# Score levels' inputs between value copies, and the order in which sparse attention opens

## The reference

```python
# branch A: gated linear attention
inter = einsum('blhk,bhkv->blhv', qb * exp(cum), state)
scores = einsum('bthk,btshk,bshk->btsh', qb, exp(cum[t] - cum[s]), kb)   # within a chunk
k_dec = kb * exp(tot - cum)
state = state * exp(tot) + einsum('blhk,blhv->bhkv', k_dec, vb)
# branch C: mLSTM over qc, kc, vc; each head ends in a norm and a gate
# branch B: sparse attention
cq, ckv = rms(cq, dsa_norm_q), rms(ckv, dsa_norm_kv)      # ranks 256 and 128
q_idx = einsum('bsr,rhd->bshd', cq, w_qi) * 32 ** -0.5    # 8 index heads of 32
I = sum_h w[t,h] * relu(q_idx[t,h] . k_idx[s])            # causal
sel = top_k(I, 128)                                       # keys of each token
p = softmax(q_lat . ckv[sel] - slope * dist);  o = p @ ckv[sel]
# then gates * branches, @ w_o, router, 6 of 64 experts a token plus a shared one
```

## Time and profile before

| | us |
|---|---|
| median of 3 runs | 1441.36 (1438.7 to 1453.93) |
| profiled execution, its own time | 1441.15 |
| its span | 1439.3 |
| PE busy | 1318.4 (92%) |
| DVE busy | 1038.8 (72%) |
| ACT busy | 778.6 (54%) |

### The profile page before, as it was taken

The page is one execution under the profiler, slowest core; times in us unless marked ns, Lnnn a source line. Parts: engine busy times, 40 slices in busy tenths (PEclk is TensorE's granted clock), DMA queues, the critical chain, the costliest instruction groups (busy, mean ns, idle before and its releaser), DMA issues.

```text
span 1439.3 us, 19410 instructions
## 1 busy us (share of the span) xinstructions
PE 1318.4 (92%) x6398; PEld 1011.6 (70%) x6398; DVE 1038.8 (72%) x1302; ACT 778.6 (54%) x952; POOL 431.0 (30%) x321
## 2 busy tenths in 40 slices
PE   4897999996898889998997999999999999999986
PEld 1586788563654458888965888788887888887842
DVE  1539685774997717444576988888988999998927
ACT  3613431433334533222314888788888888888811
POOL 1100000013221000000001666566656666665610
PEclk8999999998999999999998999999999999999998
DMA  8333312003216242334227999999999999999856
GB/s 297 102 102 124 118 59 74 29 15 109 66 60 226 74 153 85 103 99 147 73 94 259 361 383 394 383 385 367 357 373 376 347 350 359 357 370 336 309 215 252
DMA packets 126617, 314.57 MB, mean 219 GB/s; under 512 B 24229, under 2 KB 61418, under 8 KB 118122
## 3 DMA queue, kind: packets, MB, share of 16 engines
q1 hardware_dynamic: 108282, 288.73, 55.7%
q0 software_dynamic: 18288, 25.21, 4.9%
HBM read 316.49 MB, written 38.80 MB: 247 GB/s over the span
## 4 chain that ended last, share of the span: by engine, by line
PE 61%; DMA 15%; DVE 11%; issue 5%; ACT 4%; POOL 2%; SPq 1%; POOLq 0%; DVEq 0%; ACTq 0%
PE bank L898 15%; PE bank L1284 9%; PE bank L903 8%; PE bank L1312 7%; DMA arena<-h_dram,tok_of 7%; DMA ring<-in_exp_w_up 5%; PE bank L1288 4%; PE bank L1271 3%; DVE arena L2070 2%; DVE top L2069 2%; DMA arena<-in_ada_w 1%; PE bank L1353 1%; PE bank L1141 1%; POOL tok_of L780 1%; PE bank L845 1%
## 5 line engine op out<-in xcount | busy, mean ns | idle before, releaser
L2324 DVE TENSOR_TENSOR ring_parts<-ring,arena_parts 128x2048 fp32r<-128x2048 f32 x186 | 424.0, 2290 | 64.2 <-ACT arena_parts L1664 63.5
L1664 ACT ACTIVATE arena_parts<-ring 128x2048 fp32r<-128x2048 f32 x186 | 356.7, 1927 | 51.8 <-DMA ring<-in_exp_w_up 47.4
L1284 PE MATMUL bank<-arena_parts,oTA_parts 128*128 128x512 f32 x496 | 200.2, 404 | 2.9 <-DVE oTC_parts L2340 1.9
L1284 PE MATMUL bank<-arena_parts,oTC_parts 128*128 128x512 f32 x496 | 195.0, 393 | 0.0
L1312 PE MATMUL bank<-arena_parts,oTB_parts 128*128 128x512 f32 x496 | 162.2, 409 | 5.1 <-DVE ring_parts L2324 5.1
L793 POOL DMA_INDIRECT y_dram<-arena,row_of x62 | 98.6, 1591 | 183.7 <-ACT arena L1691 181.2
L898 PE MATMUL bank<-hT_parts,ring_parts 128*128 128x512 f32 x344 | 143.3, 416 | 5.4 <-ACT arena L1569 3.7
L768 POOL DMA_INDIRECT arena<-h_dram,tok_of x61 | 127.3, 2088 | 54.5 <-POOL tok_of L780 51.0
L898 PE MATMUL bank<-x_parts,ring_parts 128*128 128x512 f32 x344 | 136.7, 397 | 0.0
L1288 PE MATMUL bank<-ring_parts,oTA_parts 128*128 128x512 f32 x496 | 133.7, 392 | 0.0
L1396 ACT ACTIVATE ring_parts<-ring 128x2048 fp32r<-128x2048 f32 (+1 forms) x38 | 64.8, 1710 | 118.1 <-DMA ring<-in_w_in 71.1
(11 more groups left out here) (420 smaller groups left out, 2276.7 us busy)
## 6 DMA issues: line engine op xcount, KB each, us to landing
ring<-in_exp_w_gate SPq DMA_DIRECT2D x124, 512.0 KB, 5.3
ring<-in_exp_w_up SPq DMA_DIRECT2D x124, 512.0 KB, 9.9
ring<-in_exp_w_down SPq DMA_DIRECT2D x62, 1024.0 KB, 9.8
ring<-in_w_in SPq DMA_DIRECT2D x25, 1024.0 KB, 5.4
ring<-in_ada_w SPq DMA_DIRECT2D x16, 1024.0 KB, 5.8
arena<-in_ada_w SPq DMA_DIRECT2D x4, 2048.0 KB, 16.9
x<-in_x SPq DMA_DIRECT2D x2, 2048.0 KB, 12.6
ring<-in_w_o SPq DMA_DIRECT2D x4, 1024.0 KB, 5.0
```

The source lines that it names most:

```text
L1284: mm(out_gu, t[c][:, tile_cols(4 * k + j)], hi[:, :, j, :], start=(k == 0 and j == 0 and x_ == 0), stop=False)
L1664: A(w_hi[c][k], w_raw[c][k], ACT.Copy).then_inc(sem("gu_hi_ready" if k < 2 else "down_hi_ready"), 1)
L2324: v.tensor_tensor(w_lo[c][k], w_raw[c][k], w_hi[c][k].bitcast(F32), ALU.subtract).then_inc(sem("gu_lo_ready" if k < 2 else "down_lo_ready" ...
```

## The change

In branch A PE turns the keys between the first four value products and the last four, and pb0 follows those. DVE makes the decayed keys after two value copies and the inputs of levels 0 and 1 (and the argument of level 2) between the others and ahead of the state. ACT copies pb0 out inside its level loop, behind the split of w_ga0.

In branch C ACT squares each latent inside the head in which it is projected; msq stands in head 3, mskv behind msC3. DVE makes the query latent's norm ahead of finish_c(3) and the key latent's behind it. w_qi gets a place of its own and is loaded ahead of w_cl1. After eg00 and eg01 come wi and the index queries; eu0, ckr, uk and each further eu move to later places among the index scores, and ukT is copied by ACT in place of DVE. The diff, cut (PE's code follows the table; buffers get other addresses; the counts of some waits follow the new order):

```diff
@@ -66,9 +66,10 @@
     out += [(f"ka{f}", "ka_ready", f + 1) for f in range(2)]
-    out += [(f"va{q}{i}", "v_ready", 4 * q + i + 1) for q in range(2) for i in range(4)]
+    out += [(f"va0{i}", "v_ready", i + 1) for i in range(4)]
+    out += [(f"kd{f}", "kdr_ready", f + 1) for f in range(2)]
+    out += [(f"va1{i}", "v_ready", i + 5) for i in range(4)]
     out += [("pb0", "cond_ready", 5)]
-    out += [(f"kd{f}", "kdr_ready", f + 1) for f in range(2)]
     out += [(f"st{i}{f}", "state_ready", 2 * i + f + 1) for i in range(3) for f in range(2)]
@@ -89,6 +90,7 @@
+        out += [("msq", "root_ready", 8)] if h == 3 else []
         out += [(f"cl{h - 1}", "craw_ready", h) if h else ("kidx", "kidx_ready", 1)]
@@ -96,15 +98,17 @@
+    out += [("mskv", "root_ready", 10)]
     out += early(0, "eg")
-    out += [("msq", "root_ready", 9), ("mskv", "root_ready", 10)]
-    out += early(0, "eu")
-    out += [("wi", "wcol_ready", 1), ("uk", "ukT_ready", 1)]
-    out += [("ckr", "ckr_ready", 1)]
+    out += [("wi", "wcol_ready", 1)]
     out += [(f"qi{m}", "qi_ready", m + 1) for m in range(2)]
...
         for h in range(8):
-            out += early(i - 1, "eg") + early(i - 1, "eu") if i > 1 and h == 2 else []
+            out += [("ckr", "ckr_ready", 1)] if i == 2 and h == 0 else []
+            out += early(i - 2, "eu") if i > 1 and h == 0 else []
+            out += early(i - 1, "eg") if i > 1 and h == 2 else []
+            out += early(2, "eu") if i == 3 and h == 4 else []
+            out += [("uk", "ukT_ready", 1)] if i == 3 and h == 2 else []
             out += [(f"ix{i}{h}", "relu_ready", 8 * (i - 1) + h + 1)]
@@ -575,13 +583,18 @@
+                if name == "w_cl1":
+                    sp.wait_ge(sem("oTA_ready"), 4)
+                    sp.wait_ge(sem("mb_ready"), 3)
+                    sp.dma_start(w_qi, a["dsa_w_qi"][0].rearrange("(k p) h d -> p k (h d)", p=P)).then_inc(sem("extra_loaded"), 16)
                 if name == "wgE1":
                     sp.wait_ge(sem("oTC_ready"), 4)
...
-                    sp.dma_start(w_qi, a["dsa_w_qi"][0].rearrange("(k p) h d -> p k (h d)", p=P)).then_inc(sem("extra_loaded"), 16)
                 if name == "wg1":
@@ -934,10 +947,8 @@
                 project(f"ka{f}", "w_ka", f)
-            for q in range(2):
-                for i in range(TT):
-                    project_rows(f"va{q}{i}", f"w_va{q}", i)
-            further_condition(0)
+            for i in range(TT):
+                project_rows(f"va0{i}", "w_va0", i)
             pe.wait_ge(sem("kd_ready"), 1)
@@ -945,6 +956,9 @@
                 end(ins)
+            for i in range(TT):
+                project_rows(f"va1{i}", "w_va1", i)
+            further_condition(0)
             pe.wait_ge(sem("kdr_ready"), 2)
@@ -1438,7 +1460,6 @@
-            keep_condition("pb0", cond[0])
             def out_gate(m):
@@ -1455,6 +1476,8 @@
                     split_hi(f"w_ga{l // 2}")
+                if l == 1:
+                    keep_condition("pb0", cond[0])
                 if l >= 4:
@@ -1510,7 +1537,9 @@
                     root_c(h - 1)
-                else:
+                if h == 3:
+                    root_b(0)
+                if h == 0:
                     split_hi("w_cl1")
@@ -1524,9 +1553,13 @@
                 A(hC, b[:, :], ACT.Copy).then_inc(sem("hC_ready"), 1)
+                if h:
+                    act.wait_ge(sem("craw_ready"), h)
+                    A(sqB[:, h - 1, :], craw[:, h - 1, :], ACT.Square).then_inc(sem("squares_ready"), 1)
                 if h == 2:
...
             root_c(3)
+            root_b(1)
@@ -1542,26 +1575,27 @@
-            for n in range(3):
-                act.wait_ge(sem("craw_ready"), n + 1)
-                A(sqB[:, n, :], craw[:, n, :], ACT.Square).then_inc(sem("squares_ready"), 1)
-            for n, name in enumerate(("msq", "mskv")):
-                b = done(act, name)
-                A(rsB[:, n, :], b[:, :], ACT.Sqrt, scale=1.0 / (256, 128)[n], bias=epsc[:, 0:1]).then_inc(sem("root_ready"), 1)
             early_sigmoids(0)
-            split_hi("wgE1")
-            early_copies(0)
-            b = done(act, "ckr")
-            A(ckr, b[:, :].rearrange("p (i k) -> p i k", i=TT), ACT.Copy).then_inc(sem("ckr_ready"), 1)
             for m in range(2):
...
                 for h in range(8):
+                    if i == 2 and h == 0:
+                        split_hi("wgE1")
+                        b = done(act, "ckr")
+                        A(ckr, b[:, :].rearrange("p (i k) -> p i k", i=TT), ACT.Copy).then_inc(sem("ckr_ready"), 1)
+                        act.wait_ge(sem("cn_ready"), 2)
+                    if i > 1 and h == 0:
+                        early_copies(i - 2)
                     if i > 1 and h == 2:
...
                         split_hi(f"wgE{i}")
-                        early_copies(i - 1)
+                    if i == 3 and h == 4:
+                        early_copies(2)
+                    if i == 3 and h == 2:
+                        b = done(act, "uk")
+                        A(ukT, b[:, :].rearrange("p (i h) -> p i h", i=4), ACT.Copy).then_inc(sem("ukT_ready"), 1)
                     n = 8 * (i - 1) + h
@@ -1832,10 +1866,13 @@
-            for q in range(2):
-                for i in range(TT):
-                    b = done(dve, f"va{q}{i}")
-                    v.tensor_copy(va[:, i, 256 * q:256 * q + 256], b[:, 0:256]).then_inc(sem("v_ready"), 1)
+            def value_rows(q, i):
+                b = done(dve, f"va{q}{i}")
+                v.tensor_copy(va[:, i, 256 * q:256 * q + 256], b[:, 0:256]).then_inc(sem("v_ready"), 1)
+            value_rows(0, 0)
+            value_rows(0, 1)
             dve.wait_ge(sem("cleared"), A_CLEARED)
@@ -1880,7 +1917,16 @@
+            value_rows(0, 2)
+            value_rows(0, 3)
             level_arg(0)
+            value_rows(1, 0)
+            level_mul(0)
+            level_arg(1)
+            for i in range(1, TT):
+                value_rows(1, i)
+            level_mul(1)
+            level_arg(2)
@@ -1895,12 +1941,12 @@
                 dve.wait_ge(sem("state_ready"), 2 * i + 2)
-            for l in range(7):
-                level_mul(l)
-                if l < 6:
+            for l in range(1, 7):
+                if l > 1:
+                    level_mul(l)
+                if 1 < l < 6:
                     level_arg(l + 1)
-                if l:
-                    level_merge(l - 1)
+                level_merge(l - 1)
                 if l in (1, 3):
@@ -2028,25 +2074,27 @@
                 link(v.scalar_tensor_tensor(out=dqC, in0=hD, scalar=EPS, in1=hD, op0=ALU.mult, op1=ALU.mult))
+            def latent_norm(n):
+                dve.wait_ge(sem("root_ready"), (8, 10)[n])
+                link(v.reciprocal(rsB[n], rsB[n]))
+                for k in (0, 1) if n == 0 else (2,):
+                    ins = v.scalar_tensor_tensor(out=cn[:, k, :], in0=craw[:, k, :], scalar=par[:, 30 + k:31 + k],
+                                                 in1=rsB[n], op0=ALU.mult, op1=ALU.mult)
+                ins.then_inc(sem("cn_ready"), 1)
+            v.tensor_copy(wi0[:, :], small[32:40, :]).then_inc(sem("wi0_ready"), 1)
             variance_c(3)
+            latent_norm(0)
             finish_c(3)
             dve.wait_ge(sem("oTC_ready"), 4)
-            v.tensor_copy(wi0[:, :], small[32:40, :]).then_inc(sem("wi0_ready"), 1)
+            latent_norm(1)
             b = done(dve, "wi")
...
                             ALU.mult).then_inc(sem("wcol_ready"), 1)
-            b = done(dve, "uk")
-            v.tensor_copy(ukT, b[:, :].rearrange("p (i h) -> p i h", i=4)).then_inc(sem("ukT_ready"), 1)
-            dve.wait_ge(sem("craw_ready"), 3)
-            for n in range(2):
-                dve.wait_ge(sem("root_ready"), n + 9)
-                link(v.reciprocal(rsB[:, n, :], rsB[:, n, :]))
-                for k in (0, 1) if n == 0 else (2,):
-                    ins = v.scalar_tensor_tensor(out=cn[:, k, :], in0=craw[:, k, :], scalar=par[:, 30 + k:31 + k],
-                                                 in1=rsB[:, n, :], op0=ALU.mult, op1=ALU.mult)
-                ins.then_inc(sem("cn_ready"), 1)
             dve.wait_ge(sem("wcol_ready"), 1)
```

More of the change, by code:

```diff
@@ L1026, in _ @@
                     mean_square(h - 1)
+                if h == 3:
+                    pe.wait_ge(sem("squares_ready"), 9)
+                    b = begin("msq")
+                    for k in range(2):
+                        ins = mm(b[:, :], ones[:, :], sqB[:, k, :], start=(k == 0), stop=(k == 1))
+                    end(ins)
                 if h == 0:
@@ L1044, in _ @@
             mean_square(3)
+            pe.wait_ge(sem("squares_ready"), 11)
+            b = begin("mskv")
+            end(mm(b[:, :], ones[:, :], sqB[:, 2, :], start=True, stop=True))
             def early_gates(n):
@@ L1498, in root_c, with root_b @@
                 A(rsC, rsC, ACT.Sqrt).then_inc(sem("root_ready"), 1)
+            def root_b(n):
```

(2 more changed lines are left out.)

53 lines of the change are left out of this document (29 added, 24 removed).

## The result

The change made the kernel faster: 1424.81 us (median of 6, 1422.43 to 1432.45) against 1442.43 us for the kernel before beside it, a ratio of 0.989 (95% interval 0.986 to 0.992). I measured it twice more, on other chips: 1430.04 against 1440.70 (ratio 0.992, 0.990 to 0.994) and 1427.05 against 1444.89 (0.987, 0.985 to 0.989). The forecast was 1426 us, a ratio of 0.9895.

What follows compares the result with a forecast made beforehand. PE was taken as the bound nearly throughout, waiting on DVE in the levels and on norms at sparse attention's opening, then DVE's 82.8 us chain. -17.4 + 2.2 = -15.2 from 1441.15 gave 1426 us, range 1417 to 1436.

Steps and rivals of the forecast that it cites:

- Opening, 20.1 us earlier: Start of sparse attention: DVE's first index sum begins at 336.5 instead of 356.56, the long wait for the latents' norms gone.
- rule of eight: PE's banks: a product needs the bank of the one eight before; in the levels, level 0 waits for pb0's copy, 120.7.
- wrong if the first index sum starts after 341: Opening of sparse attention: sign that the term failed; the sum was expected near 338.7.
- Chain, 85.4 us: DVE from first index sum to first logits: 82.8 us before, plus 0.4, 1.0 and 1.2; ends 17.4 us earlier.
- the 88 I had called wrong: Sign for DVE's chain in sparse attention: wrong if it lasts over 88 us or under 83.
- hand-offs: ACT's work between the chain's relus: wgE2's split costs 0.4 us in block 2, eu2's copies 1.0 in block 3.
- 45% of its time: DVE's sums beside POOL in blocks 2 and 3: 45% of 7.5 us lost, 3.4 us for 2.2 before, cost 1.2.
- shift with the chain: Behind the chain: eu3's products, accE's store and the ada weights wait for events that move with it; no cost counted.
- each sum waits out a whole POOL instruction: Rival on DVE's chain: 7.5 us lost beside POOL and not 3.4, total 1430; chance 0.08.
- Score levels, 2.2 us later: Branch A's levels: PE waits for pb0's copy until 120.7, level 2's multiply begins at 128.0 against 125.77; bounds -1 and +5.
- Sum: Whole kernel: -17.4 + 2.2 = -15.2 us from the profiled 1441.15, giving 1426.
- The slower rival: PE at half clock to 166 behind the new 10.8 us gap, +19 us, 1460; chance 0.04.

Runs made afterwards that it cites:

- msq_later: Changed kernel with the query latent's sum of squares on PE behind the key latent's last product (cl2), not ahead of it; 1425.14 us, ratio 0.988.
- split_late: Changed kernel with ACT's split of wgE2, and POOL's half of it, behind block 2's eighth relu instead of its second; 1424.87 us, ratio 0.990.
- levels_only: Kernel before with only the change's parts in branch A's score levels, sparse attention left as it was; 1442.37 us, ratio 1.001.
- pool_fine: Changed kernel with POOL's half of the wgE2 split in 16 instructions of 128 columns instead of 4 of 512; 1424.98 us, ratio 0.989.
- all_four: Changed kernel with pb0's copy before w_ga0's split, msq behind cl2, wgE2's split behind block 2's relus, eu2's copies behind block 3's; 1413.62 us, ratio 0.978.

## Why the prediction was right, and where its terms were not

The time came out at 1424.8 for a forecast of 1426, in the forecast's own range, and the order of the causes held: sparse attention pays, the levels do not. The total flatters the terms: two of the three were too good by 2.3 to 4.4 us each, and that the time agreed all the same is in part luck.

- **Opening, 20.1 us earlier: mis-sized, 15.7 to 17.3.** (54.0 less 38.3 to 36.6.) The sum took PE to be free at 317.4 for the third square and never asked which bank cl2 would need. With msq put ahead of it, the product eight before cl2 is bm3, whose reader is DVE's last weight of head 3; it was den2. I applied the rule of eight to the levels and not here. With msq behind cl2 (msq_later) the step took 32.6 us, where the forecast had 33.9 (336.5 less 302.6). The other waits came as told: 1.52 us for the square, no wait for the queries, 3.70 us for them. My own sign for this term, wrong if the first index sum starts after 341, was met in all three profiles (341.92, 345.72 and 345.99), though these were 2.0 to 2.2 us late ahead of both changed stages.
- **Chain, 85.4 us: mis-sized, 87.7 in every profile of the changed kernel.** That lies just inside the 88 I had called wrong. The hand-offs were right: 0.54 us ahead of the third relu of block 2 for a forecast of 0.4, and 0.69 in block 3 for 1.0. The steps that failed are both of POOL. First, its "45% of its time", taken from one row of two products: in block 2's sums and the copy behind them DVE lost 4.4 us, where the forecast had 2.2. Second, a term put at nothing: eu3's products "shift with the chain". They came 9.3 us earlier (426.34, and 435.62 before), but the masking of block 3 came 11.6 us earlier (426.36, and 437.94), so they met, and it lost 2.0 us. In all, against the same parts undisturbed (block 2's sums 5.37 us in split_late, block 3's masking 1.23 in levels_only), POOL cost DVE 7.6 us of the chain after and 3.8 before, a net 3.8, where I had 3.4 and 2.2.
- **The rival "each sum waits out a whole POOL instruction"**, which I gave 0.08, had the mechanism of block 2. Its 89.5 us counted all of POOL's 7.5 us in two places; those two lost 5.5, the 2.0 at the end it didn't have, and the 3.8 of the kernel before it had as 2.2. So it too came near by luck. A sum of 0.62 us and a subtraction of 1.24 (start to start, alone) would make a beat of 1.86 if each waited the other out, and the beat was 1.54; with pieces of 0.41 us it would be 1.03, and was 0.73 in pool_fine. Both are 0.3 us short. The Trainium skill (SBUF — State Buffer, "Who interferes with whom") says that a DVE instruction with two SBUF inputs contends with a GpSimd instruction that reads SBUF, under an exclusive lock. The one-to-one order agrees, up to those 0.3 us. One reading of mine was wrong: block 2's first sum (L2061, 1.42 us for 0.41) is a TENSOR_SCALAR with one such input, so two inputs are not what all stretched instructions have in common.
- **Score levels, 2.2 us later: right in mechanism, 1.2 in levels_only** (126.94 and 125.77). The load landed after 9.6 us (109.38 to 118.99) and not 10.8; PE began at 119.72 there, forecast 120.7. In the time it is 0 within the interval, 2 us faster to 6 slower.
- **Sum.** 15.2 us were forecast. The stages as traced give 15.7 to 17.3 less 4.9 less about 1: 10 to 11 us, which the first pair of profiles agrees with (10.8 us behind their common landmark). Medians gave 17.6, 10.7 and 17.8. The profiled executions of the changed kernel lie at the upper end of its times (1432 to 1434), and what the faster ones save no trace here shows: on two of three chips some 7 us of the gain stay without a place. That cause is open.
- **The slower rival** (half clock from 130 to 166 behind the new gap) did not happen: the clock in that stretch was 1.00 in the first profile and 0.95 in the second, behind gaps of 9.83 and 10.63 us.

## What to carry to other kernels

When a product is put into a rotation of banks, look up the product eight before for it and for each one behind it, up to the next wait: here one sum of squares of 1.9 us made PE wait for 3.4 to 5.1 us that way, and 1.5 of them, seen further on as a wait of another name, were only the echo. When two vector engines hold each other up, price each meeting by the length of the other engine's instruction, and look for meetings at the end of the stage too: DVE's chain moved by 11.6 us, POOL's products behind it by 9.3, and the meeting that this made cost 1.9 us that no term had. Cut the other's instruction fine, or put it beside instructions that do not care. And when a gap has one name in the trace, ask what stands next: the copy of pb0 held 9.8 us, of which its removal gave 5 at the next landmark; what that is worth at the end, these runs can't tell.

## What the runs showed of the hardware

- MAX8 and MATCH_REPLACE kept their time beside POOL: from the end of the masking to L2119 or its like, block 2's sixteen rounds took 20.05 us before (386.39 to 406.44) and 20.05 us after (373.02 to 393.07), with 7.4 and 8.7 us of POOL's work beside them. A TENSOR_SCALAR with one input, 128x512, took 1.53 us beside POOL's product and 0.43 us in all_four, where it began 0.1 us ahead of POOL's. That fits the Trainium skill (SBUF — State Buffer, "Who interferes with whom"), which says that this operation can take the shared ports in some modes; the runs don't show the mode. COPY_PREDICATED took 1.31 us for 0.30 (128x128) and 1.67 for 0.73 (128x512).
- The granted clock differs between executions at the same instructions, with PE about as busy ahead of them. The query latent's sum (L1045, x4) took 2.70 us in the first profile of the changed kernel (clock 0.61 in 304 to 308, after 6.00 us busy of 6 at 0.98) and 1.88 in the second. By then the two were 5.4 us apart (303.64 and 309.09), with 162.45 and 162.46 us of PE work in 135 to 300 and a clock there of 0.97 and 0.94.
